# A two-layer hybrid trunk: linear attention's level products as 64x64 blocks in four quadrants of TensorE, unpadded queries, and a 16-column projection in four column groups

## The reference, cut to what matters

```python
# GLA, layer 0
q, k, v, ad, g = split_cols(ub, [GLA_KEY, GLA_KEY, MIX_HALF, GLA_GATE_RANK, MIX_HALF])   # 256, 256, 512, 16, 512
log_a = jax.nn.log_sigmoid((ad @ alpha_up + alpha_bias).astype(f32)) / GLA_GATE_NORM
o = chunked_gated_linear_attention(hd(q) * GLA_DK ** -0.5, hd(k), hd(v), hd(log_a))

# the recurrence, for GLA and HGRN2
def step(state, inp):
    qc, kc, vc, gc = inp
    b = jnp.cumsum(gc, axis=2)
    o_inter = jnp.einsum('bhid,bhdv->bhiv', qc * jnp.exp(b), state)
    diff = jnp.where(causal[:, :, None], b[:, :, :, None, :] - b[:, :, None, :, :], -jnp.inf)
    scores = jnp.einsum('bhid,bhjd,bhijd->bhij', qc, kc, jnp.exp(diff))
    o_intra = jnp.einsum('bhij,bhjv->bhiv', scores, vc)
    b_last = b[:, :, -1:, :]
    state = (jnp.exp(b_last[:, :, 0, :])[..., None] * state
             + jnp.einsum('bhjd,bhjv->bhdv', kc * jnp.exp(b_last - b), vc))
    return state, o_inter + o_intra
```

## Time and profile before

| | |
|---|---|
| median of 3 runs | 1566.76 us |
| profiled execution, its own time | 1568.86 us |
| its span, first to last instruction | 1567.1 us |
| mean granted TensorE clock | 0.948 of full |
| PE busy (matmul) | 1387.7 us, 89% |
| DVE busy | 644.1 us, 41% |
| ACT busy | 313.6 us, 20% |
| level products L1422, 512 records | 61.3 us busy |

### The profile page before, as it was taken

The page is one execution under the profiler, slowest core; times in us unless marked ns, Lnnn a source line. Parts: engine busy times, 40 slices in busy tenths (PEclk is TensorE's granted clock), DMA queues, the critical chain, the costliest instruction groups (busy, mean ns, idle before and its releaser), DMA issues.

```text
span 1567.1 us, 22853 instructions
## 1 busy us (share of the span) xinstructions
PE 1387.7 (89%) x9981; PEld 717.1 (46%) x9981; DVE 644.1 (41%) x1004; ACT 313.6 (20%) x525; POOL 77.0 (5%) x231
## 2 busy tenths in 40 slices
PE   5999999769988797899999859999998879999991
PEld 2445554347777444433333344555653353333331
DVE  1115552256665215433223245475732463233324
ACT  2220211233342103000000042432112300000002
POOL 7100000000000000000000020000000000000001
PEclk9999999979999798999999979999999889999996
DMA  9673210134542206899999661111100489999984
GB/s 360 225 268 108 101 53 7 54 137 149 163 153 95 81 0 268 355 394 400 378 424 422 283 242 54 54 55 54 54 0 1 207 348 389 424 348 426 424 358 174
DMA packets 87696, 332.63 MB, mean 212 GB/s; under 512 B 6456, under 2 KB 37420, under 8 KB 70188
## 3 DMA queue, kind: packets, MB, share of 16 engines
q1 hardware_dynamic: 74336, 290.04, 47.7%
q10 hardware_dynamic: 7788, 21.19, 3.4%
q0 software_dynamic: 5472, 19.93, 3.3%
HBM read 308.60 MB, written 22.54 MB: 211 GB/s over the span
## 4 chain that ended last, share of the span: by engine, by line
PE 70%; DVE 13%; DMA 11%; ACT 4%; issue 2%; POOL 0%; SPq 0%; DVEq 0%; ACTq 0%; POOLq 0%
PE banks L1381 16%; PE banks L1851 15%; PE banks L1872 9%; PE banks L1767 5%; DVE work L1987 5%; PE banks L1422 4%; PE banks L1370 4%; DMA h_features<-in_w_up_dram 3%; PE banks L1298 2%; DMA h_features<-in_w_down_dram 2%; PE banks L1751 2%; DMA h_features<-in_w_ada_dram 2%; DVE work L1993 1%; DMA ring<-in_w_ada_dram 1%; PE banks L1830 1%
## 5 line engine op out<-in xcount | busy, mean ns | idle before, releaser
L1381 PE MATMUL banks<-h_features,ring 128*128 128x512 f32 (+1 forms) x656 | 291.3, 600 | 5.6 <-ACT h_features L962 4.1
L1851 PE MATMUL banks<-ring,work 128*64 128x512 f32 (+1 forms) x672 | 203.8, 603 | 3.7 <-issue 2.3
L1851 PE MATMUL banks<-work 128*64 128x512 f32 (+1 forms) x672 | 199.6, 595 | 0.0
L1381 PEld LDWEIGHTS banks<-h_features,ring 128*128 128x128 f32 (+1 forms) x656 | 122.3, 190 | 156.3 <-issue 152.5
L1987 DVE TENSOR_TENSOR work<-work,banks 128x256 f32<-128x256 f32 (+2 forms) x82 | 44.8, 568 | 172.3 <-PE banks L1851 132.4
L1851 PEld LDWEIGHTS banks<-ring,work 128*64 128x64 f32 (+1 forms) x672 | 60.6, 129 | 104.0 <-issue 99.3
L1987 DVE TENSOR_TENSOR work<-work 128x512 f32<-128x512 f32 (+9 forms) x212 | 102.4, 483 | 13.3 <-ACT work L1161 3.6
L1872 PE MATMUL banks<-ring,work 128*64 128x512 f32 (+1 forms) x288 | 98.7, 593 | 3.6 <-DMA h_features<-in_w_down_dram 3.0
L1851 PEld LDWEIGHTS banks<-work 128*64 128x64 f32 (+1 forms) x672 | 59.8, 130 | 68.9 <-issue 65.4
L1767 PE MATMUL banks<-y_features,ring 128*128 128x512 f32 x192 | 85.6, 608 | 6.4 <-DVE small L2523 6.4
L847 POOL DMA_INDIRECT work<-h_rows,idx_tok x20 | 19.1, 954 | 1261.6 <-DVE idx_tok L2659 939.2
(11 more groups left out here) (369 smaller groups left out, 1803.0 us busy)
## 6 DMA issues: line engine op xcount, KB each, us to landing
ring<-in_w_up_dram SPq DMA_DIRECT2D x16, 2048.0 KB, 14.7
work<-in_w_gate_dram SPq DMA_DIRECT2D x16, 2048.0 KB, 13.7
work<-in_w_up_dram SPq DMA_DIRECT2D x14, 2048.0 KB, 13.8
h_features<-in_w_ada_dram SPq DMA_DIRECT2D x24, 1024.0 KB, 5.7
ring<-in_w_down_dram SPq DMA_DIRECT2D x12, 2048.0 KB, 13.9
work<-in_w_down_dram SPq DMA_DIRECT2D x8, 2048.0 KB, 13.7
h_features<-in_w_down_dram SPq DMA_DIRECT2D x8, 2048.0 KB, 14.0
ring<-in_w_ada_dram SPq DMA_DIRECT2D x7, 2048.0 KB, 12.6
```

What stands on the lines that cost most here:

```text
L1381: ins = mm(PS[0:w, b, :], lhsT=W[:, k, c0:c0 + w], rhs=h[:, k, :], start=(k == 0), stop=(k == KD - 1))
L1851: ins = mm(PS[rows, bank, :], lhsT=xt[:, k, rows], rhs=w[:, k, :], start=(k == 0), stop=(k == KD - 1))
```

## The change

1. **Level products.** Each 128x128 product of a level becomes 64x64 blocks. The two heads of a pair of partitions are two row halves (64 features each), the two halves of a tile's keys are two column halves. The first (diagonal) step issues 32 products with 128 query columns. Levels 1 to 32 issue 32 products with 64 columns, since queries only meet keys of their own half tile. Level 64 issues 16 products with 64 columns. The heads of the two row halves go to different banks, so the order of the 16 score tiles in PSUM and in `lA` changes.
2. **Unpadded queries.** `lqp` is 2 planes, like q. The memsets that wrote its zeros go (DVE in layer 0, POOL before layer 1), and each DVE write of `lqp` is one instruction over 128 partitions: one where there were four per level, one where there were two at SUMS and TILE_DECAYS.
3. **State reads.** In OUTPUTS the product of state and queries contracts over the head's 64 partitions (it was 128, half of it zeros).
4. **Decay input.** The `lora` block goes to four groups of 32 columns of the array, two k-blocks to each, and leaves four partial sums of 16 rows; the product with `alup` sums them, with `alup` loaded four times by four DMAs and zeros (a POOL memset at the start) between the copies. The semaphore count for the parameters rises from 9 to 12.

```diff
-        lqp = la(4, T)
+        lsq = la(4, T)
+        lqp = lsq[:, 0:2, :]
@@ POOL
+            fill(alup, 0.0)
@@ POOL, after layer 0
-                    pool.memset(lqp.rearrange("p a b -> p (a b)"), 0.0).then_inc(sem("pool_const"), 1)
@@ ACT, parameters
-            act.dma_start(alup[0:16, :], A["b_alpha_up"][0]).then_inc(sem("params_loaded"), 16)
+            for g in range(4):
+                act.dma_start(alup[32 * g:32 * g + 16, :], A["b_alpha_up"][0]).then_inc(sem("params_loaded"), 16)
@@ PE, projections
-                    elif kind == "dt":
+                    elif kind in ("dt", "lora"):
                         for k in range(KD):
                             g = k % 4
-                            ins = mm(PS[32 * g:32 * g + 32, b, :], lhsT=W[:, k, c0:c0 + w], rhs=h[:, k, :],
+                            ins = mm(PS[32 * g:32 * g + w, b, :], lhsT=W[:, k, c0:c0 + w], rhs=h[:, k, :],
                                      start=(k < 4), stop=(k >= 4))
@@ PE, level products
+                    reach = 0 if step == LEVELS else LV[step - LEVELS - 1]
                     for t in range(NT):
-                        for hd in range(4):
-                            ins = mm(PS[:, AB + t, hd * P:(hd + 1) * P], lhsT=lkp[:, hd // 2, t * P:(t + 1) * P],
-                                     rhs=lqp[:, hd, t * P:(t + 1) * P], start=True, stop=True)
+                        for j in range(2):
+                            for keys in range(2 if reach < 64 else 1):
+                                first = 0 if not reach else 64 * keys if reach < 64 else 64
+                                at, queries = t * P + 64 * keys, slice(t * P + first, (t + 1) * P if not reach else t * P + first + 64)
+                                for par in range(2):
+                                    pp = slice(64 * par, 64 * par + 64)
+                                    c = (2 * (t % 2) + j) * P
+                                    ins = mm(PS[64 * keys:64 * keys + 64, AB + 2 * (t // 2) + par, c + queries.start - t * P:c + queries.stop - t * P],
+                                             lhsT=lkp[pp, j, at:at + 64], rhs=lqp[pp, j, queries], start=True, stop=True)
@@ PE, outputs
-                            ins = mm(o, lhsT=lS[:, hd // 2, :], rhs=lqp[:, hd, t * P:(t + 1) * P],
+                            pp = slice(64 * (hd % 2), 64 * (hd % 2) + 64)
+                            ins = mm(o, lhsT=lS[pp, hd // 2, :], rhs=lqp[pp, hd // 2, t * P:(t + 1) * P],
@@ DVE, products of a level
-                for par in range(2):
-                    pp = slice(64 * par, 64 * par + 64)
-                    for t2 in range(2):
-                        q_hi = halves(lq[pp, t2, :], hh)[1]
-                        o_hi = halves(lqp[pp, 2 * t2 + par, :], hh)[1]
-                        link(tt(o_hi, q_hi, eq[pp, t2], ALU.mult))
+                link(tt(halves(f2(lqp), hh)[1], halves(f2(lq), hh)[1], eq, ALU.mult))
@@ DVE, sums
-                if l == 0:
-                    link(dve.memset(f2(lqp), 0.0))
-                for par in range(2):
-                    pp = slice(64 * par, 64 * par + 64)
-                    link(dve.tensor_copy(lqp[pp, par::2, :], lq[pp]))
+                link(dve.tensor_copy(lqp, lq))
@@ DVE, tile decays
-                for par in range(2):
-                    pp = slice(64 * par, 64 * par + 64)
-                    link(tt(lqp[pp, par::2, :], lq[pp], le2[pp], ALU.mult))
+                link(tt(f2(lqp), f2(lq), le, ALU.mult))
```

More of the change, by code:

```diff
@@ L377, in trunk @@
         lS = la(2, P)
-        lsq = lqp
         lrms = work[:, KEEP:KEEP + 4 * T].rearrange("p (a b) -> p a b", b=T)
@@ L1406, in attention @@
                 if step == LOGS and l == 0:
-                    pe.wait_ge(sem("params_loaded"), 16 * 9)
+                    pe.wait_ge(sem("params_loaded"), 16 * 12)
                     pe.wait_ge(sem("proj_copied"), 7)
                     for j in range(2):
-                        ins = mm(PS[:, AB + j, :], lhsT=alup[0:16, j * P:(j + 1) * P], rhs=le[0:16, 0:T],
+                        ins = mm(PS[:, AB + j, :], lhsT=alup[:, j * P:(j + 1) * P], rhs=le[:, 0:T],
                                  start=True, stop=True)
@@ L1439, in attention @@
                         o = PS[:, AB + hd, t * P:(t + 1) * P]
-                        ins = mm(o, lhsT=lv[:, t, hd * P:(hd + 1) * P], rhs=lA[:, 4 * t + hd, :],
+                        ins = mm(o, lhsT=lv[:, t, hd * P:(hd + 1) * P], rhs=lA[:, 8 * (t // 2) + 4 * (hd % 2) + 2 * (t % 2) + hd // 2, :],
                                  start=True, stop=(t == 0))
                         if t:
-                            ins = mm(o, lhsT=lS[:, hd // 2, :], rhs=lqp[:, hd, t * P:(t + 1) * P],
+                            pp = slice(64 * (hd % 2), 64 * (hd % 2) + 64)
+                            ins = mm(o, lhsT=lS[pp, hd // 2, :], rhs=lqp[pp, hd // 2, t * P:(t + 1) * P],
                                      start=False, stop=True)
@@ L2028, in late_parameters @@
             def late_parameters():
-                dve.wait_ge(sem("params_loaded"), 16 * 9)
+                dve.wait_ge(sem("params_loaded"), 16 * 12)
                 for par in range(2):
@@ L2082, in projections @@
                     elif kind == "lora":
-                        ins = dve.tensor_copy(le[0:16, 0:T], ps[0:16, :])
+                        ins = dve.tensor_copy(le[:, 0:T], ps)
                     elif kind == "gate":
@@ L2139, in attention @@
                 elif step == LOGS:
-                    dve.wait_ge(sem("pool_const"), 3)
+                    pass
                 elif step == SUMS:
@@ L2169, in products @@
                 dve.wait_ge(sem("lev_exp"), lev_n * l + n + 1)
-                eq = le[:, 0:512].rearrange("p (t n h) -> p t n h", t=2, h=hh)
+                eq = le[:, 0:512].rearrange("p (n h) -> p n h", h=hh)
                 ek = le[:, 512:1024].rearrange("p (n h) -> p n h", h=hh)
-                for par in range(2):
-                    pp = slice(64 * par, 64 * par + 64)
-                    for t2 in range(2):
-                        q_hi = halves(lq[pp, t2, :], hh)[1]
-                        o_hi = halves(lqp[pp, 2 * t2 + par, :], hh)[1]
-                        link(tt(o_hi, q_hi, eq[pp, t2], ALU.mult))
+                link(tt(halves(f2(lqp), hh)[1], halves(f2(lq), hh)[1], eq, ALU.mult))
                 signal(tt(halves(f2(lkp), hh)[0], halves(f2(lk), hh)[0], ek, ALU.mult), "lev_ready")
@@ L2213, in tile_decays @@
                 dve.wait_ge(sem("tile_decay"), 2 * l + 1)
-                le2 = le.rearrange("p (a b) -> p a b", b=T)
-                for par in range(2):
-                    pp = slice(64 * par, 64 * par + 64)
-                    link(tt(lqp[pp, par::2, :], lq[pp], le2[pp], ALU.mult))
+                link(tt(f2(lqp), f2(lq), le, ALU.mult))
                 link(dve.tensor_copy(ebl, le.rearrange("p (a t s) -> p a t s", a=2, s=P)[:, :, :, P - 1]))
@@ L2482, in ssd @@
                     ssd_tile(1)
-                    dve.wait_ge(sem("pool_const"), 4)
+                    dve.wait_ge(sem("pool_const"), 3)
                     ssd_scores(0)
```

## The result

The changed kernel takes 1529.35 us (median of 4 runs, 1527.06 to 1531.09), against 1567.06 (4 runs beside them, 1564.74 to 1570.59). The ratio is 0.976, 95% interval 0.9747 to 0.9772. The forecast was 1530 us, its range 1521 to 1542.

What follows compares the result with a forecast made beforehand. PE was taken to bound the level stretches. Layer 0's 22.3 us and layer 1's 15.1, together 37, took the profiled 1568.86 to 1531.9, or 1529.8 against the median; forecast 1530 us, range 1521 to 1542.

Steps and rivals of the forecast that it cites:

- Level products: PE's score products at 16 steps in two layers: 57.1 us falls to 20.2, a gain of 36.9 us.
- The rival in which quadrants take turns: Level products on PE: no two overlap, levels 1 to 32 take 3.95 us, total 1580 us; chance 3%.
- The records' pitch: Level products on PE: rounds of four records 0.058 us apart, 64 records in 1.16 us, 18 ns each.
- Lora block: Decay input on PE: the block falls from 6.96 us to 1.85, a gain of 5.1 us.
- alpha: Decay input's product with alup on PE: contracting over 128 rows no longer turns the array, gain 0.15 us.
- State reads: OUTPUTS on PE: 24 heads turn the array twice each at 0.24 us per head, 5.8 us more.
- my own sign: State reads in OUTPUTS: over 0.7 us a head would show the prediction wrong.
- The rival that turning is dear: State reads and levels on PE: a turn costs 0.35 us, total 1548 us; chance 8%.
- The clock: Both level stretches on PE: granted clock falls to the run's mean 0.948, costing 9 us, total 1539; chance 8%.
- Waits of DVE: PE's waits: KEYS_TURNED gains 1.2 us in layer 0, 0.8 in layer 1; layer 1's levels lose 1.3, SSD squares 0.2.
- The walk for layer 0: ACT and DVE chain before KEYS_TURNED: about 7.1 to 7.3 us against PE's 6.87, leaving 0.5 us of waiting.
- The five stretches: PE from projections to RWKV-7 in layer 0 and to the out projection in layer 1: predicted 37.4 us gained.

Runs made afterwards that it cites:

- E5: Level products as full 128x128 products again, against the changed kernel; 1562.73 us, ratio 0.9975 to the kernel before.
- E6: The changed kernel's 64x64 level products reordered, all of one quadrant and then the next; 1567.54 us, ratio 1.0008 to the kernel before.
- E4: The lora block and its product with alup as before, all else as in the changed kernel; 1535.87 us, ratio 0.9817 to the kernel before.
- E2: The changed kernel with state reads over all 128 partitions again, each mixing two heads; 1522.55 us, ratio 0.9702 to the kernel before.
- E9: The changed kernel with value products and state reads grouped by pairs of heads, four turns a tile; 1521.27 us, ratio 0.9708 to the kernel before.
- E3: The changed kernel with four value products first, then the four state reads, two turns a tile; 1514.8 us, ratio 0.9665 to the kernel before.
- E7: The changed kernel with DVE's multiplication of the queries in four instructions per level again; 1533.51 us, ratio 0.9796 to the kernel before.
- E1: The changed kernel measured again without any edit; 1532.32 us, ratio 0.9777 to the kernel before.
- E10: Four value products, then state reads in head order 0, 2, 1, 3, otherwise as the changed kernel; 1515.67 us, ratio 0.9675 to the kernel before.
- E11: Four value products, then four state reads over all 128 partitions, otherwise as the changed kernel; 1514.9 us, ratio 0.966 to the kernel before.

## Why the prediction was right, and where its steps were off

- **Level products: right in mechanism, about 0.1 us a level too cheap.** Predicted 1.15 us, 2.05 for the first step, 1.15 for level 64, each with its turns. Measured 1.09, 1.91 and 1.08 from start to start, but part of the turns stands in the blocks around, 0.19 a block, so the level to set against 1.15 is 1.28. In layer 0 the eight steps gave about 18.0 us, not 18.7. The stretch's 20.03 looks like a hit because it also holds 1.3 us of the wait at KEYS_TURNED and 0.7 of a v block that ran at a higher clock (7.67 us before, 6.97 after, start to start). E5 shows that the levels carry the gain, E6 that it comes from the order. The rival in which quadrants take turns named a real price: E6 comes near that kernel. Its level costs 3.33 us, not 3.95.
- **The records' pitch: right.** The 64 records of a level take 1.09 us, 17 ns each. The 62 ns that the Trainium skill ("TensorE: Matmul & The Clock Gate", section "Wait — 56ns, not 53.3ns?") states for hardware decode off do not bind these products; by them a level would have taken an estimated 4.0 us.
- **Lora block: right in mechanism, 1.3 to 2 us short.** The block and alpha gave 5.2 as forecast. What I left out is the clock behind the old block and its small products, 0.66 in the trace of before, where the change has 1.00 (E4).
- **State reads: the term that was mis-sized.** I took 0.12 us a turn and 5.8 us in all. A turn between alternating short products is 0.193 (0.386 per head, E2 and E9), and the alternation costs 8.3 us at full clock. The bound of 0.5 per head held it; the value came from turns next to full blocks, which are the wrong neighbour for products of 0.22 us. With the clock's fall, 4.5 us, the reads cost 12.8 us (E2), more than twice the 5.8 of the sum. By my own sign (over 0.7 us a head; measured 0.83) this step was wrong. The rival that turning is dear had 0.35 us a turn; what was measured lies between. The Trainium skill's "TensorEngine Tiling (Array Packing)", section "Key Properties", says that a change of tiling mode drains the engine; the estimate of at least 0.16 and about 8 us that I had worked out for that was nearer than my own value. The rows agree with it in size; that a drain is what the 0.19 us are, no run here shows.
- **The clock: a rival that came at another place.** I looked for a fall in the stretches of the levels. There it stayed at 1.00 in layer 0 and is 0.97 in layer 1 (0.96 before). It fell in the state reads of layer 0, for a loss of about 4.5 us, and it does not fall there with two or four turns a tile (E3, E9) or none (E2). I had argued that no new pause was longer than 1.3 us. None was needed: the wait of 0.91 us before the fall stands in E3 too, at clock 1.00.
- **Waits of DVE: right.** Level 64 of layer 1: 0.94 (predicted 1.2). KEYS_TURNED: 1.42 in layer 1 (1.6) and none in layer 0 (0.5). The walk for layer 0 was added up wrongly: its terms make 6.74 us, not 7.1 to 7.3, and that is less than PE's 6.87. SSD squares 3.92 (3.84 + 0.2). E7 confirms that DVE's shorter work is worth something in layer 1 only.
- **RWKV-7's first product: 291.25, predicted about 289.** The 2 us are the state reads' 6.1 too much, less the gains of lora and of the start.
- **Why the total came out all the same.** The five stretches gave 31.9 us, not 37.4. The first medians differ by 37.7, and E1's ratio makes 34.9. What lies between, some 3 to 6 us, stands in stretches that the change does not touch. The 327.11 us of before from layer 1's experts to the end are longer than the 322.56 to 325.58 of all twelve others. PE is busy for as long in it as after (281.8 and 282.3 us), so the difference is waiting and not the clock; with one profile of before I can't say whether the change has a part in it. This stays open. The mechanisms were right, but that 1530 met 1529.35 so closely is in part luck: these few us offset the mis-sized state reads.

## What to carry to other kernels

Cutting a matmul into 64x64 blocks pays only if neighbouring products go to different quadrants, and then threefold (1.09 against 3.33 us for the same products). Each change between full array and part of it costs about 0.2 us between short products, so group products by tiling mode (the part of the array that they use) before anything else: that alone took the changed kernel from 1532.3 to 1514.8 us, with some 6 us of that from falls of the clock that did not come. When you price a product from the trace, look for a row with the same shape and the same neighbours: next to a long block a turn costs only about 0.1 us. And measure a stage together with the block behind it, since part of its cost may stand there.

## What the hardware showed that I had not expected

- Alternating full-array and 64-row products for 3.2 us at full clock was followed by a granted clock of 0.50 for about 10 us (an estimate from the windows after), at the same place in layer 0 in all six profiles with this code, with PE busy all the while but for a wait of 0.91 us. In E3 the same stretch, with the same wait, stays at 1.00, and so does the same alternation in layer 1, where a block stands between the tiles. What in it brings the fall on was not separated.
- A full-length block of 16 columns, 7 us, and 5 us of small products behind it were followed by a clock of 0.66 to 0.79, which cost nearly 2 us in the rows behind (E4 and the kernel before).
- Two row halves overlap even where two products on one half stand in a row: four reads 0.65 us in the order 0, 1, 2, 3 and in 0, 2, 1, 3, and 0.99 over the full array (E3, E10, E11).
- Stretches with identical code differ by up to 6.7 us with the granted clock (224.57 us at 0.94 and 231.28 at 0.91 from RWKV-7 to the out projection).
